# Both mixing stages in a new order, gate products inside two input units, identity products between head products

## What is computed

```
h = layer_norm(x)                                   # 256 tokens x 1024
for l in 0, 1:
    proj = h @ w_in[l]                              # 1024 x 3088
    y = concat(retention(proj), s5(proj), hyena(proj), mlstm(proj))   # 4 heads of 64 or 256 channels each
    h = layer_norm(DN_ALPHA * h + y @ w_out[l])
    f = swiglu(h) if l == 0 else top-2-of-8 experts(h)
    h = layer_norm(DN_ALPHA * h + f)
```

## Time and profile before

| what | us |
|---|---|
| median of three runs | 1684.67 |
| the profiled execution | 1687.43 |
| its span, first to last instruction | 1685.6 |
| PE busy over the span | 1631.7 (97%) |
| DVE busy | 1355.8 (80%) |
| ACT busy | 945.7 (56%) |
| POOL busy | 55.5 (3%) |

### The profile page before, as it was taken

One profiled execution on the slowest core, in us unless ns is written; L12 is line 12 of the kernel. 1 busy time (PEld: TensorE's weight loads), 2 busy tenths in 40 slices (PEclk: granted clock), 3 DMA queues, 4 the chain that ended last, 5 costly groups with the idle time before them and its releaser, 6 DMA issues.

```text
span 1685.6 us, 18495 instructions
## 1 busy us (share of the span) xinstructions
PE 1631.7 (97%) x7566; PEld 1272.5 (75%) x7566; DVE 1355.8 (80%) x1447; ACT 945.7 (56%) x961; POOL 55.5 (3%) x39
## 2 busy tenths in 40 slices
PE   7898999999999999999999999999999999999996
PEld 4555758988857666788888888888888888888885
DVE  6989456765566855788988998888898988998897
ACT  4312415654311132677767767777777777777773
POOL 0111000000011010000000000000000000000000
PEclk9998989999999988999999999999999999999998
DMA  8221152743443114599988999988999989999981
GB/s 325 93 100 50 75 217 96 268 186 150 153 172 150 50 49 186 230 376 371 371 356 335 369 357 373 369 344 344 366 363 374 360 338 360 386 361 374 361 337 49
DMA packets 40604, 444.24 MB, mean 264 GB/s; under 512 B 4416, under 2 KB 4544, under 8 KB 7360
## 3 DMA queue, kind: packets, MB, share of 16 engines
q1 hardware_dynamic: 39360, 438.78, 66.8%
q10 hardware_dynamic: 1152, 4.19, 0.6%
HBM read 437.71 MB, written 5.24 MB: 263 GB/s over the span
## 4 chain that ended last, share of the span: by engine, by line
PE 82%; DVE 12%; ACT 3%; issue 1%; DMA 1%; SPq 0%; DVEq 0%; ACTq 0%
PE bank L1113 33%; PE bank L1140 15%; PE bank L992 8%; PE bank L606 4%; PE bank L1001 4%; PE bank L813 3%; PE bank L610 3%; DVE ring_lo L2028 2%; PE bank L1121 1%; PE bank L775 1%; DVE ring_lo L2158 1%; ACT ex_up_hi L1404 1%; PE bank L749 1%; DMA pr<-par 1%; PE bank L1061 1%
## 5 line engine op out<-in xcount | busy, mean ns | idle before, releaser
L2028 DVE TENSOR_TENSOR ring_lo<-ring,ex_up_hi 128x2048 fp32r<-128x2048 f32 x224 | 512.9, 2290 | 51.4 <-ACT ex_up_hi L1404 49.8
L1404 ACT ACTIVATE ex_up_hi<-ring 128x2048 fp32r<-128x2048 f32 x224 | 429.1, 1916 | 113.9 <-PE bank L1113 106.2
L1113 PE MATMUL bank<-ex_up_hi,ex_x_hi 128*128 128x512 f32 x896 | 362.5, 405 | 6.2 <-DVE ring_lo L2028 4.7
L1113 PE MATMUL bank<-ring_lo,ex_x_hi 128*128 128x512 f32 x896 | 350.7, 391 | 0.0
L1113 PE MATMUL bank<-ex_up_hi,ex_x_lo 128*128 128x512 f32 x896 | 349.9, 390 | 0.0
L2158 DVE TENSOR_TENSOR ring_lo<-ring,ex_w_hi 128x2048 fp32r<-128x2048 f32 x111 | 253.2, 2281 | 0.0
L1512 ACT ACTIVATE ex_w_hi<-ring 128x2048 fp32r<-128x2048 f32 x111 | 211.4, 1905 | 0.0
L1113 PEld LDWEIGHTS bank<-ex_up_hi,ex_x_hi 128*128 128x128 f32 x896 | 168.3, 188 | 44.4 <-DVE ring_lo L2028 13.7
L1113 PEld LDWEIGHTS bank<-ring_lo,ex_x_hi 128*128 128x128 f32 x896 | 168.1, 188 | 36.7
L1113 PEld LDWEIGHTS bank<-ex_up_hi,ex_x_lo 128*128 128x128 f32 x896 | 168.8, 188 | 30.6
L1140 PE MATMUL bank<-ex_w_hi,ex_mid_hi 128*128 128x512 f32 x448 | 174.5, 389 | 0.0
(11 more groups left out here) (329 smaller groups left out, 2121.6 us busy)
## 6 DMA issues: line engine op xcount, KB each, us to landing
ring<-moe SPq DMA_DIRECT2D x112, 2048.0 KB, 7.6
ring<-moe SPq DMA_DIRECT2D x112, 1024.0 KB, 7.4
ring<-ffn SPq DMA_DIRECT2D x11, 3072.0 KB, 10.9
win<-w_in SPq DMA_DIRECT2D x12, 2048.0 KB, 8.4
win<-w_out SPq DMA_DIRECT2D x4, 2048.0 KB, 10.8
lnb<-ln SPq DMA_DIRECT2D x4, 1024.0 KB, 5.9
tab<-yT ACTq DMA_DIRECT2D x8, 512.0 KB, 5.3
pr<-par SPq DMA_DIRECT2D x2, 1728.0 KB, 11.4
```

Source lines behind the costliest of these rows:

```text
L1113: ins = mm(b[:, :], ex_x[x % 3][x_][:, k, :], (ex_up_hi, lo)[w_][:, k, :], start=(k == 0 and m == 0), stop=(k == KT - 1 and m == 2))
L1404: act(ex_up_hi[:, HS * q:HS * (q + 1), :], wt[:, HS * q:HS * (q + 1), :], ACT.Copy).then_inc(e_uh, 1)
L2028: tt(ring_lo[s][:, half], ring[s][:, half], hi.bitcast(F32), ALU.subtract).then_inc(e_ul, 1)
```

## The change

Unit 12 is gone from the list of units. Its products are made inside units 8 and 9, each ahead of the unit's own product with the same stationary tile, into bank 4; these two units wait for the parameters, and in layer 1 for the third spectrum product. DVE's `gates` follows unit 9 in place of unit 12, and units 6 and 7 use banks 5 and 6. The calls of all six lists are put in another order. Between the calls at the end of PE's lists stand calls of `keep_busy`: seven in `mix_0` (26 products) and six in `mix_1` (24 products), into the last 128 columns of banks 4 and 6.

```diff
-UNITS = (0, 8, 9, 10, 11, 1, 2, 3, 12, 6, 7, 4, 5)
+UNITS = (0, 8, 9, 10, 11, 1, 2, 3, 6, 7, 4, 5)
-UNIT_BANK = (5, 6, 5, 6, 5, 6, 5, 6, 5, 6, 5, 1, 2)
+UNIT_BANK = (5, 6, 5, 6, 5, 6, 5, 6, 5, 6, 1, 2)
...
-                    mm(bank[b][:, 0:P], ident, ident, start=True, stop=True)
+                    mm(bank[b][:, 384:512], ident, ident, start=True, stop=True)
...
+                    with_gates = i in (8, 9)
+                    gw = W("gate_w").rearrange("p (k n) -> p k n", k=KT)
+                    if with_gates:
+                        pe.wait_ge(s_par, 16 * (l + 1))
+                        if l:
+                            pe.wait_ge(f_spec, 4 * l + 3)
                     for k in range(KT):
+                        x = hT[:, k, part * P:(part + 1) * P]
+                        if with_gates:
+                            mm(bank[4][:, part * 16:(part + 1) * 16], x, gw[:, k, :], start=(k == 0), stop=(k == KT - 1))
+                        ins = mm(b[:, :], x, w[:, k, :], start=(k == 0), stop=(k == KT - 1))
...
```

PE's list of layer 1, the end of the diff:

```diff
+                out_product(1, "hyena", 3)
                 ml_scores(1, 0)
-                out_product(1, "hyena", 3)
+                s5_glu(1)
+                keep_busy(4, 6)
                 head_out(2, 4)
-                s5_glu(1)
+                out_product(1, "s5", 3)
+                keep_busy(4, 6)
+                ml_scores(1, 1)
                 out_product(1, "ret", 3)
-                ml_scores(1, 1)
                 ml_out(1, 0)
-                out_product(1, "s5", 3)
+                keep_busy(4, 4)
                 ml_scores(1, 2)
+                keep_busy(4, 4)
                 ml_out(1, 1)
+                keep_busy(4, 4)
+                keep_busy(4, 4)
                 ml_scores(1, 3)
+                out_product(1, "hyena", 0)
                 ml_out(1, 2)
+                out_product(1, "ret", 2)
+                ml_out(1, 3)
...
```

More of the change, by code:

```diff
@@ L596, in unit @@
                     pe.wait_ge(f_spec, 4 * l + p + 1)
[L597 to L601, removed]
+                j, part = next((j, w[1].index(i)) for j, w in enumerate(WIN_LOADS) if i in w[1])
+                s, v = win_use(l, j)
+                pe.wait_ge(win_in[s], v)
+                w = win[s][:, :].rearrange("p (k n) -> p k n", k=KT)
                 if i < 6:
@@ L607, in unit @@
                                      start=(k == 0), stop=(k == KT - 1))
-                elif i < 12:
-                    for k in range(KT):
[L610 to L617, removed]
+                else:
+                    with_gates = i in (8, 9)
[4 more added lines that the diff above has]
+                            pe.wait_ge(f_spec, 4 * l + 3)
+                    for k in range(KT):
+                        x = hT[:, k, part * P:(part + 1) * P]
+                        if with_gates:
+                            mm(bank[4][:, part * 16:(part + 1) * 16], x, gw[:, k, :], start=(k == 0), stop=(k == KT - 1))
+                        ins = mm(b[:, :], x, w[:, k, :], start=(k == 0), stop=(k == KT - 1))
                 ins.then_inc(pj, 1)
@@ L827, in mix_0 @@
                 unit(0, 11)
+                pre(0, 0)
+                unit(0, 1)
+                pre(0, 1)
                 s5_in(0, 2)
-                unit(0, 1)
-                pre(0, 0)
                 unit(0, 2)
-                pre(0, 1)
+                s5_in(0, 3)
+                pre(0, 2)
                 unit(0, 3)
-                pre(0, 2)
-                s5_in(0, 3)
                 pre(0, 3)
+                s5_in(0, 4)
+                pre(0, 4)
                 s5_y(0, 1)
-                pre(0, 4)
+                pre(0, 5)
                 s5_y(0, 2)
-                pre(0, 5)
-                s5_in(0, 4)
-                unit(0, 12)
+                ml_gate_rows(0, 0)
                 unit(0, 6)
@@ L847, in mix_0 @@
                 pre(0, 7)
+                ml_gate_rows(0, 1)
                 pre(0, 8)
+                unit(0, 7)
+                pre(0, 9)
                 s5_y(0, 4)
                 s5_in(0, 6)
-                pre(0, 9)
                 pre(0, 10)
-                ml_gate_rows(0, 0)
-                unit(0, 7)
+                ml_columns(0)
                 hyena_transposes(0, 0)
-                ml_gate_rows(0, 1)
+                hyena_forward(0, 0)
+                ret_transposes(0)
@@ L870, in mix_0 @@
+                hyena_inverse(0, 0)
+                hyena_transposes(0, 1)
+                ret_out(0, 0)
+                hyena_forward(0, 1)
+                ret_scores(0, 2)
+                ret_out(0, 1)
+                ret_scores(0, 3)
+                s5_y(0, 6)
+                ret_out(0, 2)
                 s5_y(0, 7)
                 unit(0, 4)
-                ret_out(0, 1)
-                ret_scores(0, 3)
-                ret_out(0, 2)
+                ret_out(0, 3)
+                keep_busy(2, 6)
@@ L913, in mix_1 @@
                 unit(1, 10)
+                s5_y(1, 0)
                 s5_in(1, 2)
```

180 lines of the change are left out of this document (85 added, 95 removed).

## The result

The changed kernel takes 1670.86 us (median of 4 runs, 1669.8 to 1674.4), the kernel before 1685.21 us beside it (4 runs, 1684.57 to 1687.12): a ratio of 0.9914, interval 0.9899 to 0.993. It is 14.4 us faster; the forecast was 8.7 us and 1676.0 us, rival B 17.7 us and 1667.

What follows compares the result with a forecast made beforehand. PE was taken as the bound, 45.6 us above its own work, with DVE's chain first in stage 0. Gains of 8.9 (stage 0) and 8.8 us (stage 1), less 9.0 for low clock, gave 8.7: 1676.0 us, range 1667 to 1692.

Steps and rivals of the forecast that it cites:

- rival B: Whole kernel: the clock holds at full level everywhere, 17.7 us gained, 1667 us; chance 0.20.
- Part 1: Gate products inside units 8 and 9: no change of work, the gate unit's half clock goes, 3.2 us a stage.
- Part 2: Stage 0 up to the last S5 scan: DVE's chain bounds it, that scan ends at 159.9 instead of 162.9 us.
- -8.8 and +5.9: DVE's chain in stage 0: waits of 5.8 and 3.0 us go (-8.8); new waits for filter products and crossings come (+5.9).
- The new wait at the second filter step: DVE in stage 0: waits for PE's product behind unit 1, +3.7 us.
- the tenths at each crossing: DVE in stage 0: some tenths at each new crossing, 1.3 us in all.
- Part 3: Rest of stage 0, from the last S5 output product: tail 71.6 instead of 75.8 us; stage 0 gains 8.9 us.
- Part 5: Clock staying low in the mLSTM loops: half of their 18.0 us loss stays, taking 9.0 us off the gain.
- the uncovered evacuation: Ahead of the last four output products: PE waits for ACT's 0.84 us evacuation, +1.1 us with the hop, in each stage.
- Part 4: Stage 1, PE the bound throughout: 16.5 us of wait and half clock go, 7.7 are added, gain 8.8 us.
- Rival A: Both mLSTM loops: identity products do not hold the clock, 8.4 us slower, 1693 us; chance 0.18.
- C: Rival on DVE's chain in stage 0: not shorter, and 13.5 us of half clock stay; about 1683.5 us; chance 0.14.

Runs made afterwards that it cites:

- the repeat: The changed kernel run once more, unaltered, as base for later runs: 1672.53 us, ratio 0.9915 to the kernel before.
- the spread kernel: Changed kernel without the 50 identity products, its three bank-3 output products standing one by one between the heads: 1665.56 us, ratio 0.9872 to the kernel before.

## Why the prediction was right, and where it was not

**The mechanism.** PE's order and clock were the bound, the gate units' half clock went, stage 0 got shorter, and the loops' clock rose. The result lies in the forecast's own range, 1670 to 1681, but 0.9 us from its lower end and nearer to rival B's 1667 than to 1676.0: the parts were right in kind, while the middle of the range was not.

**Part 1 is shown.** 8.74 us for a unit with gates is 1.7 us more, 3.4 us a layer; the old unit, 5.66 us at a mean clock of 0.63, is some 3.6 us at full clock. So there was hardly a change of work, and the gate unit's half clock went in both stages when this was changed alone. That the same edit would also shorten the half clock of stage 1's loop was not seen.

**Part 2 was 2.3 us too careful.** DVE's waits up to the last scan fall from 14.1 to 9.2 us, 4.9, where the prediction's -8.8 and +5.9 give 2.9. The new wait at the second filter step is 3.5 us (3.7 forecast) and the later one 1.1; the tenths at each crossing did not come, and two short waits of 0.4 and 0.2 us went. The work itself is 0.5 us shorter (0.1 forecast). The Hyena gate's second product takes 2.03 us beside POOL's addition; with POOL at rest it took 0.69 (before, from 155.9 us), so it loses 1.3 where 1.5 was costed. The reciprocal stands directly behind scan 4, beside the same kind of addition, at 3.35 us as with POOL at rest: 0 was right. The Trainium skill (SBUF — State Buffer, "Who interferes with whom"), by which it does not contend, agrees with this row.

**Part 3's tail is right to 0.2 us, with Part 5 left out.** From the start of the last S5 output product (160.76) to the stage's end it is 71.8 us, forecast 71.6. Identity instructions are 0.118 us (0.116), the uncovered evacuation 0.93 (1.1).

**Part 4 missed 1.9 us.** PE's first Hyena output wait is gone, the 48 identity instructions take 5.8 us, the uncovered evacuation 0.9, no half clock is left; that makes 16.5 - 6.7 = 9.8 us with small waits at nothing, and 6.9 were measured. Two causes give 1.6 of the 2.9 us between. The half clock and the waits were added up as if they stood apart, but 1.2 us of the half clock lay within waits (from 613.33 to 620.15 us PE is busy for 5.60 of 6.82): 0.6 us was counted twice. And a term was left out: in the old order two groups of score products followed each other and ran together. From PE's timeline of the kernel before:

```profile
533.99 1.91 PE L775 MATMUL bank<-ring,pr 128*32 128x256 f32 x8
535.83 4.85 PE L616 MATMUL bank<-pr,hT 128*128 128x16 f32 x32
...
581.25 1.14 PE L679 MATMUL bank<-ret 64*128 64x256 f32 x8
```

From the changed kernel, where other products stand between:

```profile
529.03 1.91 PE L774 MATMUL bank<-ring,pr 128*32 128x256 f32 x8
530.88 0.60 PE L700 MATMUL bank<-cst,small 128*4 128x128 f32 x4
...
566.88 1.13 PE L678 MATMUL bank<-ret 64*128 64x256 f32 x4
567.93 1.12 PE L761 MATMUL bank<-uT,pr 32*128 32x256 f32 x4
568.99 1.13 PE L678 MATMUL bank<-ret 64*128 64x256 f32 x4
```

Eight score instructions in 1.1 us are now two times four in 1.05 each (567.93 - 566.88), 1.0 us more. The other 1.3 us are spread in tenths over PE's other groups and small waits, and are not traced further. Two S5 output groups also run together when they follow each other; in stage 1 of the kernel before they did not, as the gate unit stood between (second row), but they do in the kernel with the gate products alone:

```profile
534.85 2.81 PE L774 MATMUL bank<-ring,pr 128*32 128x256 f32 x16
```

Sixteen in 2.8 us against two times eight in 1.85 each (530.88 - 529.03) is 0.9 us. With the 1.0 us of the scores it is most of the 2.6 us that the new order, without identity products, loses there against the gate products alone. No run changes these neighbours alone, so this is read from rows and not tested. The Trainium skill (TensorE: Matmul & The Clock Gate, "Part 3: Packing small matmuls — row/col tiling") says that small products at different row or column places of the array run at the same time; these rows agree in kind.

**The step that failed is Part 5.** "I take half of the loss as staying, 9.0" was wrong: in the changed kernel both loops stand at 1.00, and nothing of the 18.0 us stays there. The reason given, that the products between the narrow ones are wide ones only in part, is not borne out: half as many identity products were still enough in the profile of that run. Rival B therefore describes the profiled execution to the tenth (17.7 us), partly by chance, since +1.4 us in stage 0 and -1.9 in stage 1 nearly cancel. By the medians the gain is 14.4 us, between the two: other executions have half clock at other places, as the repeat has in the router's part (3.4 us) and as the mean clocks of the ten executions show. What decides where it falls stays open. Rival A is refuted (1.00 in the loops, 0.118 us an instruction), and so is C (last scan at 157.65 us).

**What the parts are worth.** By ratios, the gate products give 0.64%. The new order without identity products adds nothing measurable to that (0.9949 against 0.9936): 7.5 us gained in stage 0, most of it by the clock, but 2.6 lost in stage 1 and 3.4 behind it. The identity products on top give 0.35%; at full number they cost about as much as the clock they hold in stage 0. Half of them came out lower (0.9888), and so did wide products that the stage needs anyway, without any added work (0.9872); between these two the intervals do not decide.

## What to carry to other kernels

Before instructions are added to hold a clock, look for work that is due anyway and can stand in the gaps; if none is free, try the smallest number that holds it in several executions, for most of them are paid for unless a wait is shown at that place (here 4.0 of 5.8 us). Sum a reordering by groups of neighbours, not only by calls: products that ran side by side lose that when something is put between them. Where half clock wanders from run to run, read a stage's length only together with its stretches at half clock, compare executions at an equal mean clock, and judge by several runs.

## What the runs showed of the hardware

- Identity products of 128 columns hold TensorE at its full level (2.4 GHz, granted clock 1.00) between products of 65 and 256 columns, at 0.116 to 0.118 us an instruction; half as many did too in one run, and in another with the same list of stage 1 left 3.4 us at 0.50. One a place beside spread wide products held it in the loop of stage 0 (1.00) and not in that of stage 1 (6.8 us at 0.52, around a wait of 3.0 us).
- The half level (1.2 GHz) began in waits of PE (of 5.3 and 3.0 us in the spread kernel), but also while PE had work without a gap: the router's part, identity products among its own, ran at 0.51 for 6.8 us in one run of the change and at the full level in another. So identity products do not hold the clock everywhere.
- Where half clock falls differs between executions of one kernel: six of the change had a mean clock of 0.993 (1669.8 to 1671.1 us), four 0.990 (1674.4 to 1675.3 us).
- Small products of the same kind in direct succession take 0.18 us an instruction instead of 0.23 (S5 outputs) and 0.13 to 0.14 instead of 0.26 (scores).
- DVE's reciprocal (3.35 us) is not slowed by a GpSimd addition beside it, while the Hyena gate's product of two inputs takes 2.03 us with 1.5 us of it beside one, 1.02 us with only its first 0.5 us beside one, and 0.69 us with GpSimd at rest.
